# Low parts of the down weights: a negated copy and an accumulating transfer in place of a VectorE subtraction

## What is computed

```
h  = rmsnorm(x, norm_pre_ffn)
ff = silu(h @ w_gate) * (h @ w_up)          # 512 x 2816
ff = ff @ w_down                            # w_down: 2816 x 1024
x  = x + rmsnorm(ff, norm_post_ffn)
```

## Time and profile before

| what | value |
|---|---|
| median of 3 runs | 683.4 us (682.91 to 684.96) |
| the profiled execution's own time | 684.04 us |
| its span, first to last instruction | 682.2 us |
| mean granted TensorE clock | 0.998 |
| the down stage, PE's matmuls | from 553.7 to 677.0 us |

### The profile page before, as it was taken

How to read it: one execution, slowest core, us unless ns; L and a number is a source line. 1 busy time by engine, 2 the same in 40 slices (tenths; PEclk the granted TensorE clock), 3 DMA queues, 4 the chain that set the end, 5 groups by cost and what they waited for, 6 DMA issues and landing times.

```text
span 682.2 us, 10174 instructions
## 1 busy us (share of the span) xinstructions
PE 668.2 (98%) x4113; PEld 596.9 (87%) x4113; DVE 480.4 (70%) x657; ACT 320.0 (47%) x513; POOL 95.5 (14%) x130
## 2 busy tenths in 40 slices
PE   8999999999999999999899999999999989999996
PEld 6878888888988889888898999999999988888885
DVE  5766999998778778347886888888888653423325
ACT  5656334443159577235543655555546352231312
POOL 3800310000405377002300000000000000000000
PEclk9999999999999999999999999999999999999999
DMA  8453032432521302160222332332332223322303
GB/s 269 125 160 120 2 122 76 138 127 62 186 63 61 124 2 86 58 206 22 62 63 82 105 117 70 123 124 69 117 125 84 102 96 121 123 85 101 118 6 124
DMA packets 49376, 68.71 MB, mean 101 GB/s; under 512 B 5041, under 2 KB 39857, under 8 KB 49330
## 3 DMA queue, kind: packets, MB, share of 16 engines
q1 hardware_dynamic: 45760, 60.16, 27.5%
q0 software_dynamic: 3280, 7.35, 3.1%
q10 hardware_dynamic: 290, 0.55, 0.2%
HBM read 65.40 MB, written 4.74 MB: 103 GB/s over the span
## 4 chain that ended last, share of the span: by engine, by line
PE 92%; DVE 3%; ACT 2%; issue 1%; POOL 0%; DMA 0%; DVEq 0%; POOLq 0%; ACTq 0%
PE PS L1438 52%; PE PS L1769 26%; PE PS L1650 2%; PE PS L1512 2%; PE PS L1549 1%; PE PS L1488 1%; PE PS L1487 1%; PE PS L1661 1%; DVE A L1270 1%; ACT A L828 1%; PE PS L1584 1%; PE PS L1482 1%; PE PS L1536 1%; DVE A L1264 1%; PE PS L1575 1%
## 5 line engine op out<-in xcount | busy, mean ns | idle before, releaser
L1438 PE MATMUL PS<-hT_lo,w_hi 128*128 128x512 f32 (+2 forms) x280 | 101.9, 364 | 0.0
L1438 PE MATMUL PS<-hT_hi,w_lo 128*128 128x512 f32 (+2 forms) x280 | 100.6, 359 | 0.0
L1438 PE MATMUL PS<-hT_hi,w_hi 128*128 128x512 f32 (+2 forms) x280 | 100.6, 359 | 0.0
L1370 DVE TENSOR_TENSOR W_r<-W_f,s_w 128x2048 fp32r<-128x2048 f32 x11 | 25.2, 2293 | 64.0 <-ACT s_w L885 64.0
L1438 PE MATMUL PS<-s_w,ff_lo 128*128 128x512 f32 x176 | 68.5, 389 | 0.0
L973 DVE TENSOR_TENSOR w_lo<-raw,w_hi 128x2048 fp32r<-128x2048 f32 x21 | 48.1, 2293 | 20.2 <-ACT w_hi L652 20.0
L1769 PE MATMUL PS<-hT_hi,W_r 128*128 128x256 f32 x216 | 61.1, 283 | 0.0
L1769 PE MATMUL PS<-hT_hi,s_w 128*128 128x256 f32 x216 | 61.1, 283 | 0.0
L1769 PE MATMUL PS<-hT_lo,s_w 128*128 128x256 f32 x216 | 61.1, 283 | 0.0
L1438 PEld LDWEIGHTS PS<-hT_hi,w_hi 128*128 128x128 f32 (+1 forms) x280 | 52.5, 188 | 8.4
L1438 PEld LDWEIGHTS PS<-hT_lo,w_hi 128*128 128x128 f32 (+1 forms) x280 | 52.6, 188 | 7.4 <-issue 0.2
(11 more groups left out here) (246 smaller groups left out, 1655.9 us busy)
## 6 DMA issues: line engine op xcount, KB each, us to landing
raw<-in_w_in_dram SPq DMA_DIRECT2D x15, 1024.0 KB, 5.6
W_f<-in_w_down_dram SPq DMA_DIRECT2D x11, 1024.0 KB, 4.9
W_f<-in_w_gate_dram SPq DMA_DIRECT2D x9, 1024.0 KB, 5.3
W_f<-in_w_up_dram SPq DMA_DIRECT2D x9, 1024.0 KB, 5.3
raw<-in_w_o_dram SPq DMA_DIRECT2D x4, 1024.0 KB, 4.9
A<-in_x_dram SPq DMA_DIRECT2D x4, 512.0 KB, 5.8
A<-in_x_dram POOLq DMA_DIRECT2D x4, 512.0 KB, 5.4
raw<-in_w_gate_dram SPq DMA_DIRECT2D x2, 1024.0 KB, 5.4
```

What stands on the lines that cost most here:

```text
L1370: dve.tensor_tensor(lo, view(ring3(NS + d), J_DN + d), hi.bitcast(F32), ALU.subtract).then_inc(s_dlo, 1)
L1438: o = pe.matmul(out, lhs[a], rhs[b], start=(first and n == 0), stop=(last and n == 2))
```

## The change

Chunk 0 stays as it was. For chunks 1 to 10 VectorE's subtraction is gone. After the high part ScalarE writes its negative into the raw slot, and POOL then issues a transfer that reads the chunk from DRAM a second time and adds it onto the slot, so that the slot holds raw minus high. The load of the gains on POOL moves behind the first of these transfers. PE waits for the landing of each transfer on one of three semaphores.

```diff
@@ semaphores
-        s_dlo = sem("down_lo_ready")
+        s_dlo = sem("first_down_lo_ready")
+        s_dneg = sem("down_hi_negated")
+        s_dacc = [sem(f"down_lo_accumulated{i}") for i in range(3)]
@@ POOL
-            pool.wait_ge(s_gu2, 2 * NS)
-            pool.dma_start(gain_out, norm_post_ffn[0, :].partition_broadcast(P)).then_inc(s_go, 16)
+            for d in range(1, FT // 2):
+                pool.wait_ge(s_dneg, d)
+                pool.dma_start(down_split(d)[1], raw_src(J_DN + d), accum_op=ALU.add).then_inc(s_dacc[(NS + d) % 3], 16)
+                if d == 1:
+                    pool.wait_ge(s_gu2, 2 * NS)
+                    pool.dma_start(gain_out, norm_post_ffn[0, :].partition_broadcast(P)).then_inc(s_go, 16)
@@ ScalarE, down_hi
                 act.activation(down_split(d)[0], view(ring3(NS + d), J_DN + d), ACT.Copy).then_inc(s_dhi, 1)
+                if d:
+                    act.wait_ge(s_dhi, d + 1)
+                    act.activation(down_split(d)[1], down_split(d)[0].bitcast(F32), ACT.Copy, scale=-1.0).then_inc(s_dneg, 1)
@@ VectorE
             for d in range(1, FT // 2):
                 ff_lo_pair(d)
-                down_lo(d)
@@ PE
+            def down_landed(d):
+                if d == 0:
+                    pe.wait_ge(s_dlo, 1)
+                else:
+                    m = (NS + d) % 3
+                    pe.wait_ge(s_dacc[m], 16 * sum((NS + e) % 3 == m for e in range(1, d + 1)))
...
-                pe.wait_ge(s_dlo, c + 1)
+                down_landed(c)
...
-            pe.wait_ge(s_dlo, C_LAST)
+            down_landed(C_LAST - 1)
...
-            pe.wait_ge(s_dlo, C_LAST + 1)
+            down_landed(C_LAST)
```

## The result

The changed kernel took 710.08 us (median of 4 runs, 707.0 to 711.01) against 684.18 us for the kernel before in the same comparison. The ratio is 1.0368 with a 95% interval of 1.0343 to 1.0393: slower, as forecast. The forecast was 704 us, with a range of 690 to 724. The profiled execution took 709.71 us, 25.67 more than the 684.04 of the one before.

What follows compares the result with a forecast made beforehand. PE's unbroken down-stage matmuls were taken as the bound. Waits of 18.9 us plus 2.0 for clock restarts gave 20.9 us on the profiled 684.04, which was 0.64 above the median: 704.3, rounded to 704 us, range 690 to 724.

Steps and rivals of the forecast that it cites:

- PE as the bound, VectorE's subtractions worth nothing: Down stage: only PE is on the chain, so removing ten VectorE subtractions of 2.29 us each gains 0.
- ScalarE's copy, 1.92 us, and POOL's 0.30 us to the issue: Down stage, chunks 1 to 10: each negated copy takes 1.92 us, then POOL needs 0.30 us to start its issue.
- The landing, D = 8.6 us: Accumulating 1 MB transfer on POOL: 8.6 us from issue to landing, with ends of 4.7 and 16.7 us.
- The short landing: Rival: transfers land in 4.8 to 7.5 us, mostly chunks 1 and 10 wait, 688 to 697 us; chance 0.3.
- The long landing: Rival: transfers take over 10.5 us to land, adding 28 us and more, 743 us at 16.7; chance 0.2.
- Not slower, or not doing what it says: Two rivals at 683.4 us: transfers hidden, chance 0.03; or semaphore counts met early so PE doesn't wait, chance 0.02.
- The reloads and the gains, nothing: SP's chunk reloads and POOL's later load of the last norm's gains: 0, at most a few tenths for reloads.
- The waits, 18.9 us: PE before down chunks: 4.84 us at chunk 1, 2.15 each at 3, 5, 7 and 9, 5.44 at 10.
- the alternation: Down chunks 2 to 9: a late chunk gives its successor as much slack, so only every second one waits.
- The clock, 2 us: PE after the waits of 4.8 and 5.4 us: two likely restarts at 1.2 GHz, 1 us each.
- the sum: Down stage: 18.9 us of waits plus 2.0 for the clock, 20.9 us on the profiled execution's 684.04 us.

Runs made afterwards that it cites:

- both edits: Changed kernel with three places for the high parts instead of two and chunks 1 and 10 back on VectorE's subtraction: 685.88 us, ratio to before 1.0012.

## Why the prediction was right, and where a term was off

- **PE as the bound, VectorE's subtractions worth nothing:** right. The run with both edits has eight of them fewer and is no faster than before.
- **ScalarE's copy, 1.92 us, and POOL's 0.30 us to the issue:** right to about a hundredth (the copy starts at 561.08, the issue at 563.31 for chunk 1).
- **The landing, D = 8.6 us:** right at 8.4 in the median, and the reason given, two operands, fits the engines' time, which the plain load on POOL shows nearly doubled by adding. The row that carried it was the one with as many bytes to *fetch*, the load of x in the earlier trace rows; the row with as many bytes to write would have given 4.9. That it came within 0.2 us is in part luck: 1.7 of the 8.6 us are the distance between the first and the last of four issues, and the accumulating transfer has one. Its 8.4 are made up otherwise, of the plain 5.3, the longer issue and the engines' 2.7.
- **Two rivals fall by it.** The short landing is what a plain transfer gives (5.3 us and 693 us, inside its 688 to 697); the accumulating one isn't short. The long landing didn't come.
- **Not slower, or not doing what it says:** chunk 10's transfer would have had to land within 1.0 us and took 8.55; PE waited for the landings, so the counts hold.
- **The reloads and the gains, nothing:** right for PE's time, though not for the transfers. Chunk 3's reload was issued at 567.25, with chunk 1's transfer in flight, and took 9.0 us, the gains took 11.3 and chunk 2's transfer 9.9. It cost nothing because chunk 2 had slack: its transfer landed at 581.39, and PE came to it at 584.79.
- **The waits, 18.9 us:** found 19.5, at the chunks named, in the alternation named. Chunk 3's was 0.85 longer, those of chunks 5, 7 and 9 some 0.25 shorter, those of 1 and 10 as much longer. Chunks 1 and 10 on VectorE moved them to the even chunks, as the alternation demands.
- **The clock, 2 us:** the step that failed. It was forecast as "1 us for each" of two restarts and cost 6.3 us in three. Chunk 3's wait came to 3.0 us and brought a third restart, and a restart cost 1.8 to 2.7 us, not 1. With PE kept busy through those waits this loss went. The term is 4.3 of the 4.8 us by which the profiled execution exceeds the sum. Nor is it a fixed size: of the four executions the one of 707.0 us had a mean granted clock of 0.991 and the one of 711.01 us 0.984. The prediction compared each wait with a pause of 1.8 us; the length alone doesn't tell, since in the plain load on SP the clock fell after 2.1 us and not after 3.7.

## What to carry to other kernels

Work that is off the chain, as VectorE's subtractions were here, gains nothing when it is removed; what replaces it is judged by the latency from the release of its input to its result, against the time until the consumer wants it, and chunks with less cover than the others (here the first and the interleaved last) must be worked out one by one. Price an accumulating transfer at nearly twice the engine time of a plain one of its size (5.9 against 3.2 us here). Where PE has to wait some microseconds, add what the matmuls after the wait may lose at the lower clock: here it was a quarter of the whole loss.

## What the runs showed of the hardware

- The clock's restart: chunk 1's wait of 5.1 us was followed by 1.76 us of loss, chunk 10's of 5.7 us by 2.74. In the same profile it stayed at 1.00 after waits of 1.9 us. The wait's length alone doesn't decide it: with the copy made twice the clock fell after chunk 7's wait of 3.5 us and not after chunk 5's of 3.7, and with the plain load on SP after chunk 1's of 2.1 and not after chunk 10's of 3.7.
- Matmuls at 1.2 GHz cover a transfer too. Where the next wait is for a transfer already released, what they lose can come back: with the copy made twice chunk 9's lost 1.7 us, and chunk 10's wait was 2.1 us shorter.
- An accumulating megabyte occupied the DMA engines for 5.9 us where a plain one took 3.2. With three places for the high parts, one of them in flight and a plain reload issued 1.8 us behind it took 10.7 and 10.35 us, where each by itself takes 8.4 and 5.0.
